# Loading a unit of cached keys in eight 128-partition transfers instead of four 32-partition ones

## The reference

```python
def sample_attend(l):
    def attend(q, k, v, lam):
        pk = cache_k[l][page_table].reshape(dec_batch, past_len, H_DIFF, 2 * QK_HEAD_DIM)
        pv = cache_v[l][page_table].reshape(dec_batch, past_len, H_DIFF, V_HEAD_DIM)
        k_all = jnp.concatenate([pk.astype(k.dtype), k], axis=1)
        ...
        return diff_attn_core(q, k_all, v_all, qpos, kpos, rel_bias, lam)
```

## Time and profile before

| what | value |
|---|---|
| median of 3 runs | 1327.76 us (1327.72 to 1328.27) |
| the profiled execution: its own time / its span | 1327.3 us / 1325.6 us |
| TensorE busy | 1311.1 us, 99% of the span |
| VectorE / ScalarE / GpSimd busy | 55% / 34% / 12% |
| granted TensorE clock | 0.999 |
| moved by DMA | 146.96 MB, mean 111 GB/s |

### The profile page before, as it was taken

The page is one execution under the profiler, slowest core; times in us unless marked ns, Lnnn a source line. Parts: engine busy times, 40 slices in busy tenths (PEclk is TensorE's granted clock), DMA queues, the critical chain, the costliest instruction groups (busy, mean ns, idle before and its releaser), DMA issues.

```text
span 1325.6 us, 21890 instructions
## 1 busy us (share of the span) xinstructions
PE 1311.1 (99%) x8364; PEld 1190.0 (90%) x8364; DVE 726.3 (55%) x1185; ACT 446.8 (34%) x764; POOL 158.2 (12%) x323
## 2 busy tenths in 40 slices
PE   8999999999999999999999999999999999999998
PEld 7999999977667888998989898999989898989986
DVE  6446745268886655556453545455354636453556
ACT  6321001057777443441322232232303131323332
POOL 2027000022222211200000000000000000000003
PEclk9999999999999999999999999999999999999999
DMA  7676778369996241420111102010202011020117
GB/s 246 213 262 232 261 230 214 74 176 261 263 271 218 93 142 50 120 80 17 63 32 56 39 16 79 16 63 16 79 16 74 21 63 32 27 68 16 48 49 139
DMA packets 132424, 146.96 MB, mean 111 GB/s; under 512 B 25852, under 2 KB 101285, under 8 KB 132357
## 3 DMA queue, kind: packets, MB, share of 16 engines
q1 hardware_dynamic: 107865, 122.30, 31.4%
q10 hardware_dynamic: 23500, 20.24, 4.7%
q0 software_dynamic: 992, 3.54, 1.6%
HBM read 114.06 MB, written 31.47 MB: 110 GB/s over the span
## 4 chain that ended last, share of the span: by engine, by line
PE 94%; ACT 1%; DVE 1%; issue 1%; POOL 1%; DMA 0%; SPq 0%; POOLq 0%; DVEq 0%; ACTq 0%
PE PS L2521 40%; PE PS L2239 18%; PE PS L2586 17%; PE PS L2465 7%; PE PS L2289 2%; PE PS L2601 2%; PE PS L2616 2%; PE PS L2329 1%; PE PS L2316 1%; PE PS L2392 1%; PE PS L2362 1%; PE PS L2224 1%; PE PS L2456 1%; PE PS L2372 1%; ACT prob L1102 1%
## 5 line engine op out<-in xcount | busy, mean ns | idle before, releaser
L2521 PE MATMUL PS<-act_lo,wu_hi 128*128 128x364 f32 (+1 forms) x1056 | 346.4, 328 | 0.0
L2521 PE MATMUL PS<-act_hi,wu_lo 128*128 128x364 f32 (+1 forms) x1056 | 346.0, 328 | 0.0
L2521 PE MATMUL PS<-act_hi,wu_hi 128*128 128x364 f32 (+1 forms) x1056 | 345.9, 328 | 0.0
L2521 PEld LDWEIGHTS PS<-act_hi,wu_hi 128*128 128x128 f32 x1056 | 198.5, 188 | 0.5
L2521 PEld LDWEIGHTS PS<-act_lo,wu_hi 128*128 128x128 f32 x1056 | 198.1, 188 | 0.4
L2521 PEld LDWEIGHTS PS<-act_hi,wu_lo 128*128 128x128 f32 x1056 | 198.3, 188 | 0.0
L2004 DVE TENSOR_TENSOR y_acc<-y_acc,PS 128x512 f32<-128x512 f32 x162 | 111.1, 686 | 116.0 <-PE PS L2586 116.0
L2586 PE MATMUL PS<-wd_hi,g_hi 128*128 128x512 f32 x324 | 130.0, 401 | 0.0
L2586 PE MATMUL PS<-wd_lo,g_hi 128*128 128x512 f32 x324 | 128.0, 395 | 0.0
L2586 PE MATMUL PS<-wd_hi,g_lo 128*128 128x512 f32 x288 | 114.0, 396 | 0.0
L1364 ACT CAST g_hi<-conv 128x1088 fp32r<-128x1088 f32 x21 | 23.2, 1102 | 245.6 <-PE PS L2586 189.6
(11 more groups left out here) (294 smaller groups left out, 2293.6 us busy)
## 6 DMA issues: line engine op xcount, KB each, us to landing
wu_raw<-in_w_up_dram SPq DMA_DIRECT2D x44, 512.0 KB, 3.9
k_tok<-in_cache_k_dram SPq DMA_DIRECT2D x64, 256.0 KB, 4.0
keys_t<-k_turned ACTq DMA_DIRECT2D x32, 512.0 KB, 4.3
vpage<-in_cache_v_dram SPq DMA_DIRECT2D x64, 256.0 KB, 5.5
wd_raw<-in_w_down_dram SPq DMA_DIRECT2D x22, 512.0 KB, 5.3
w_raw<-in_w_in_dram SPq DMA_DIRECT2D x20, 512.0 KB, 6.5
kt_mid<-keys_t SPq DMA_DIRECT2D x20, 256.0 KB, 8.7
kt_b<-keys_t SPq DMA_DIRECT2D x20, 256.0 KB, 9.1
```

The costliest lines, as they stand in the source:

```text
L2521: mm = nc.tensor.matmul(PS[:, 3 * half + c, 0:kept(c)], a[:, half, k, :], b[:, k, KEPT[c]], start=(j == 0), stop=(j == len(parts) - 1))
```

## The change

`load_keys` issues eight transfers for a unit where it issued four. Before, transfer j took quarter j of the partitions (32 of them), and for each partition eight runs of 1 KB, one for each pair n and each i. Now, transfer (n, i) takes all 128 partitions with one run of 1 KB each. Bytes, runs and places are the same. The semaphore counts double, since twice as many transfers add 16 each.

```diff
     def kt_count(u):
 
-        return 64 * (sum(kt_place(v) == kt_place(u) for v in range(u)) + 1)
+        return 128 * (sum(kt_place(v) == kt_place(u) for v in range(u)) + 1)
...
         def load_keys(u):
 
             if u in (2, 3):
-                sp.wait_ge(kt_loaded[u - 2], 64)
+                sp.wait_ge(kt_loaded[u - 2], 128)
             if u >= 5:
                 sp.wait_ge(sscore_ready, 2 * (u - 3) + 2)
-            for j in range(4):
-                src = bass.AP(keys_t, (2 * u * 4 * 32 * 4 + j) * 256, [[4 * 256, 32], [32 * 4 * 256, 8], [1, 256]])
-                dst = kt[u][32 * j:32 * j + 32].rearrange("a n i p h t -> a (n i) (p h t)")
-                sp.dma_start(dst, src).then_inc(kt_loaded[kt_place(u)], 16)
+            for n in range(2):
+                for i in range(4):
+                    src = keys_t[2 * u + n, i].rearrange("d j c -> j d c")
+                    sp.dma_start(kt[u][:, n, i].rearrange("a p h t -> a (p h t)"), src).then_inc(kt_loaded[kt_place(u)], 16)
```

## The result

The changed kernel takes 1407.3 us (median of 4 runs, 1406.93 to 1408.89), the kernel before 1328.01 us (1327.72 to 1328.58). The ratio is 1.0599 with a 95% interval from 1.058 to 1.0617, and the medians lie 79.3 us apart. The forecast was 1423 us.

A forecast was written before the change was run, and what follows sets the result against it. TensorE, busy 99% of the span, was taken as the bound. Loads of 164 + 49 + 8 + 2 - 8 = 215 us make unit 15 89 us late; 1327.3 + 89 + 4 + 2 = 1422, 1423 against the median; range 1385 to 1525.

The forecast's parts named there:

- TensorE waits nowhere for keys, so only lateness can tell: Key multiplication: TensorE never waited for a key transfer; at most 3.3 us to win there.
- Four engines of sixteen, by the 4 outermost of the source: Key loads: the new source's 4 outermost put each transfer on 4 of 16 engines; 1423 us, chance 0.70.
- the share of 0.43 for `st_nat`: Earlier trace: a load with 8 outermost in its source was taken to run on about half of the engines.
- The engines' rate: Key loads: one engine moves 24.4 GB/s, four 97.5, so a unit takes at least 10.75 us.
- The tenth for collisions: Key loads: about a tenth added for engines meeting in memory, 11.7 us a unit, 164 us for 14 units.
- Rival 2: Key loads: four engines collide in the memory, 18.7 us a unit, 1521 us; chance 0.14.
- The values, `w_out` and the ends: Loads ahead of unit 15: 49 us for values, 8 for `w_out` rows, 2 for first packet and landing.
- lookahead: SyncE's issuing of values ahead behind a full queue: could hide 16 us, half taken, 8 us off the sum.
- What comes behind unit 15: After the last key unit: 4 us for the output projection's first tiles, 2 us for a lowered clock.
- Where the lateness shows: Key multiplication, line 2362: TensorE waits for DMA of `keys_t` for some 90 us.
- Rival 4: Key loads: half of the engines, or the issue cost alone on short slacks, 1330 to 1345 us; chance 0.05.

The follow-up runs named there:

- e6: Against e2: one transfer of 1 MB a unit, 128 partitions with eight runs of 1 KB, instead of eight transfers; 1327.95 us.
- e3: Against e2: a pad of 1 KB behind every 32 runs in the DRAM tensor, so the source can't merge and has 4 outermost; 1407.28 us.
- e2: Against the changed kernel: DRAM key tensor laid out so each transfer's source merges into 128 outermost, with stores split in four a pair; 1327.55 us.
- e5: Against the changed kernel: sixteen transfers a unit, each of 64 partitions with one run and 2 outermost in the source; 1555.48 us.
- e1: Against the changed kernel: still eight transfers a unit, but each of 32 partitions with four runs, 32 outermost on both sides; 1332.03 us.
- e4: Against the kernel before: the change made for units 0, 1 and 15 alone; 1333.23 us.

## Why the prediction was right, point by point

- **TensorE waits nowhere for keys, so only lateness can tell** held: e6 makes the loads much faster and the time stays.
- **Four engines of sixteen, by the 4 outermost of the source**: shown. e3 against e2 differs by one pad and its effect on the source pattern: 0.28 of share against 0.79, 79.7 us. e5 halves rate and share once more, and the small packets, 16, 4 and 2 to a transfer, give the number of engines. The rule of the Trainium skill, "DMA: Bandwidth & Descriptors", section "Why a DMA increments its semaphore by 16 and not by 1", gives 16, 4 and 2 engines for e2, e3 and e5; the traces agree, with 245 (held by SyncE's issues), 96 and 49 GB/s. All of these counts divide the 128 or 64 of the other side, so no run here tells that rule from one that takes the smaller of the two counts.
- **The evidence for it was weaker than it looked**: the share of 0.43 for `st_nat` need not come from half of the engines. SyncE takes 3.94 us to issue these six transfers, 0.36 MB, which is 91 GB/s in the mean, so its issuing alone would keep the rate low on any number of engines. The conclusion was right all the same. The DMA updates a transfer's semaphore 16 times in e2, 5 times in the changed kernel and 3 times in e5, which is one for each engine and one more where there are fewer than 16; the six `st_nat` transfers have 50 updates, which is 9 for each of the five with 8 outermost and 5 for the last, which has 4. But the row alone did not show it; that it pointed the right way was in part luck.
- **The engines' rate**: 24.4 GB/s from `bias_sb`, measured 24.2. The lower bound of 10.75 us a unit was nearly the value (10.84).
- **The tenth for collisions was the term that was mis-sized**: I took 11.7 us a unit, and there was nothing to add. 14 x 0.86 = 12 us of the forecast's excess. Rival 2, four engines that collide, had no part: 10.84 us and not 18.7.
- **The values, `w_out` and the ends**: I had 49 + 8 + 2 - 8 = 51 us between the keys. From 278.44 to unit 15's reading at 480.67 are 202.2 us; less 14 x 10.84 = 151.8 leaves 50.4. That the sums agree within 1 us is partly luck, as the parts differ: SyncE issued the fourteen units in 133.8 us, 18 less than the engines took, where I allowed 8 for its lookahead; the issues of `w_out` took 4.1, not 8; and 8.4 us of gaps and 6.9 from the last issue to the reading stand where I had 2 for the ends. The values took the 49 us that I had.
- **What comes behind unit 15**: 4 + 2 us were allowed for `w_out` and the clock. The span grew by 79.9 us and unit 15 was 76.5 late, so it was 3.4. From the reading of unit 15 to the output projection's first matmul it is 5.33 us instead of 4.09, with a granted clock of 0.50 in the first 2.1 of them: about 1.2 us for the clock. Behind it TensorE waits 1.6 us for ScalarE at 492.64. For `w_out` it has no wait of its own; the rest was not followed.
- Together: 12.7 us too much up to unit 15 and 2.6 behind it, 15 us, the distance from 1422 to the profiled execution's 1407.25.
- **Where the lateness shows**: the waits for keys are 60.2 us and not some 90. The pauses let the clock fall (0.83 in the mean of the stage, against 1.00), so TensorE did its work between two units slower and waited less for the next. The unit's landing sets the pace, so this moves time from waiting to working; SyncE waited for TensorE's reading of a unit only 0.6 us in the whole stage, so the slower work held up no load.
- **Rival 4's issue cost** did not show by itself: the doubled issues cost nothing in e2, and e1's waits of 3.2 us came with transfers that are slower as well.

That 32 partitions at a time slowed the transfers of the kernel before was argued from the earlier trace rows. The runs fit it: 224 GB/s there and 225 in e1, both into 32 partitions, against 355 in e6 into 128. They do not isolate it, as e6 also reads its keys from another layout in DRAM. The Trainium skill, "SBUF — State Buffer", section "Door 1: The DMA port swizzle", lets partitions 0 to 31 reach 8 of 16 ports, by which the rate would be, as an estimate, one half of the full one; the trace has 0.63 of e6's. No run here looked at single ports.

## What to carry to other kernels

Before reshaping a transfer, write down the outermost count of both of its sides as they stand after merging: a permuted source ("j d" of a tensor stored as "d j") can put a 4 in front of 128 partitions and leave twelve of sixteen engines idle. The sign in a profile is a low DMA share with a rate in proportion, while SyncE stands in its issues; lay the DRAM side out so that the outer dimensions merge. And count a load's slack from the end of the queue ahead of it, not from its own issue.

## What the runs showed of the hardware

- Four engines carried 1 KB packets at 24.2 GB/s each (the changed kernel, 10.84 us a unit), two at 24.1 (e5). With all 16 at work it was 22.2 in e6 (355/16) and some 24.4 for `bias_sb`.
- SyncE's issue of a transfer takes 0.47 us in an empty queue (e2). In a full one it takes as long as the engines take to carry a transfer: 1.355 us for 131 KB on four engines, 1.358 us for 65 KB on two. A slow transfer so holds up every load that stands behind it in the list: from 286 to 308 us the DMA share was 0.27, with the first values waiting in the list until 309.22.
- In the longer pauses the granted clock fell from 1.00 to 0.50. Sixteen of the key matmuls took 1.94 us behind pauses of 7.29 us (unit 5) and 3.77 us (unit 15 in e4), and eight took 1.08 us instead of 0.64 behind 4.74 us (unit 3); behind 1.96 us (unit 15 in e1) sixteen took 1.07 us, as without a pause. Of the 3.4 us behind unit 15 the clock cost about 1.2.
